# Differential attention and the latent branch's merge as one stage in half tiles, on one Trainium2 core

## The reference

```
z = h @ w_in                      # among others q_d, k_d, v_d and three gates of 1024 columns
p  = softmax(q_d[...,0] . k_d[...,0]) - lam * softmax(q_d[...,1] . k_d[...,1])   # 4 heads, 64 columns per map
o_d = rms(p @ v_d) * g * (1 - lam_init)                                           # per head of 128
y = sig(gate_m) * (o_m @ w_m) + sig(gate_a) * (o_a @ w_a) + sig(gate_d) * (o_d @ w_d)
x = x + g1 * (y @ w_out)          # then an MLP with squared ReLU
```

## Time and profile before

| what | value |
|---|---|
| median of three runs | 2680.42 us |
| profiled execution | 2682.99 us, span 2681.1 us, mean granted clock 0.983 |
| TensorE busy | 2559.7 us, 95% |
| VectorE busy | 1180.7 us, 44% |
| ScalarE busy | 744.2 us, 28% |
| GpSimd busy | 1330.8 us, 50% |
| da, layer 0 and layer 1 | from 585.2 and 1896.3 us, about 76 us each |

### The profile page before, as it was taken

How to read it: one execution, slowest core, us unless ns; L and a number is a source line. 1 busy time by engine, 2 the same in 40 slices (tenths; PEclk the granted TensorE clock), 3 DMA queues, 4 the chain that set the end, 5 groups by cost and what they waited for, 6 DMA issues and landing times.

```text
span 2681.1 us, 41661 instructions
## 1 busy us (share of the span) xinstructions
PE 2559.7 (95%) x17328; PEld 2394.0 (89%) x17328; DVE 1180.7 (44%) x1692; ACT 744.2 (28%) x1332; POOL 1330.8 (50%) x604
## 2 busy tenths in 40 slices
PE   4999989999999999999989999899999999999997
PEld 3989976877999999999978899668789999999997
DVE  4443265777224523132554523659742273132233
ACT  3251235225312312021222522450433123021121
POOL 2635530340566666666654356105236666666664
PEclk8999999999999999999998999999999999999999
DMA  6202224530222222222211122342012222222221
GB/s 249 70 24 70 73 79 158 195 111 9 72 71 71 71 79 72 77 73 73 78 55 55 32 74 71 117 158 79 32 40 71 73 70 71 79 72 78 72 78 57
DMA packets 62555, 215.33 MB, mean 80 GB/s; under 512 B 6688, under 2 KB 11168, under 8 KB 62112
## 3 DMA queue, kind: packets, MB, share of 16 engines
q1 hardware_dynamic: 56448, 203.97, 22.3%
q10 hardware_dynamic: 5920, 8.70, 0.9%
HBM read 208.15 MB, written 4.49 MB: 79 GB/s over the span
## 4 chain that ended last, share of the span: by engine, by line
PE 83%; DVE 8%; issue 3%; ACT 1%; DVEq 1%; POOL 1%; DMA 1%; SPq 1%; POOLq 0%; ACTq 0%
PE big L469 22%; PE big L473 22%; PE big L472 22%; PE big L620 4%; PE last_two L651 2%; PE two L634 2%; PE last_two L547 1%; PE big L493 1%; DVE cols L1377 1%; PE big L496 1%; PE big L497 1%; DMA first_mod<-in_first 1%; DVE sq L1720 1%; SPq L380 1%; DVE q_a L1684 1%
## 5 line engine op out<-in xcount | busy, mean ns | idle before, releaser
L437 POOL TENSOR_TENSOR w_hi<-raw,cst 128x1024 fp32r<-128x1024 f32 x288 | 556.1, 1931 | 1219.9 <-PE big L469 1106.8
L469 PE MATMUL big<-act_hi,w_hi 128*128 128x320 f32 x2784 | 870.5, 313 | 6.9 <-issue 5.6
L472 PE MATMUL big<-act_lo,w_hi 128*128 128x320 f32 x2784 | 864.5, 311 | 0.0
L473 PE MATMUL big<-act_hi,w_lo 128*128 128x320 f32 x2784 | 864.1, 310 | 0.0
L440 POOL TENSOR_TENSOR w_lo<-raw,w_hi 128x1024 fp32r<-128x1024 f32 x288 | 744.1, 2584 | 41.0
L469 PEld LDWEIGHTS big<-act_hi,w_hi 128*128 128x128 f32 x2784 | 526.6, 189 | 16.6 <-issue 14.8
L472 PEld LDWEIGHTS big<-act_lo,w_hi 128*128 128x128 f32 x2784 | 526.6, 189 | 1.0
L473 PEld LDWEIGHTS big<-act_hi,w_lo 128*128 128x128 f32 x2784 | 526.4, 189 | 0.0
L469 PE MATMUL big<-u_hi,w_hi 128*128 128x320 f32 (+1 forms) x1024 | 319.0, 312 | 2.0 <-DVE u_lo L1783 2.0
L472 PE MATMUL big<-u_lo,w_hi 128*128 128x320 f32 (+1 forms) x1024 | 317.4, 310 | 0.0
L473 PE MATMUL big<-u_hi,w_lo 128*128 128x320 f32 (+1 forms) x1024 | 317.0, 310 | 0.0
(11 more groups left out here) (306 smaller groups left out, 3456.9 us busy)
## 6 DMA issues: line engine op xcount, KB each, us to landing
raw<-in_w SPq DMA_DIRECT2D x368, 512.0 KB, 3.5
first_mod<-in_first SPq DMA_DIRECT2D x16, 512.0 KB, 15.8
x<-in_x ACTq DMA_DIRECT2D x1, 2560.0 KB, 12.9
out_y<-x SPq DMA_DIRECT2D x8, 320.0 KB, 2.3
cst<-in_const ACTq DMA_DIRECT2D x1, 1664.0 KB, 10.3
small<-in_small ACTq DMA_DIRECT2D x2, 437.0 KB, 9.5
out_C<-c_new ACTq DMA_DIRECT2D x2, 258.0 KB
v_d<-in_past ACTq DMA_DIRECT2D x2, 256.0 KB, 3.1
```

The lines of the kernel that those rows point to most:

```text
L437: nc.gpsimd.tensor_tensor(w_hi[:, to, :], raw[:, slot, :], ones[:, 0:1].to_broadcast([P, BLK]), ALU.mult)
L469: first = mm(ps, wh, ah, start=k == 0, stop=False)
L472: mm(ps, wh, al, start=False, stop=False)
L473: last = mm(ps, wl, ah, start=False, stop=k == nk - 1)
```

## The change

- merge_a is no stage of its own any more. Its 576 products are cut into half tiles: an item is one gate tile's half of 320 tokens (24 products) or one branch tile's half (12 products). They go to two PSUM banks of their own, one per half (`half_banks`). The products are dealt out over 42 slots: two ahead of and between the first scores, then two per unit.
- da gets its own loops on all engines (`attend_d`). Per unit TensorE makes the scores of unit i+1, a slot, the transposes of unit i, a slot, the values of unit i. The scores read 64 rows of q_d and k_d directly, the two maps alternating; q_map, its zeros and `lay_out` are gone. Transposes and values share two further banks, and VectorE copies each unit's output at once (`out_copied`).
- ScalarE takes tanh of each gate half in da (`half_gates`), VectorE multiplies and adds each branch half there (`half_branches`).
- The squares of the heads stand in da, in four tiles (`head_sq`). The sums, roots, scaling and splits stand beside the first gates of merge_d (`head_roots` for two heads at once). merge_d's order is four gates, four branch tiles, then twice two gates and two branch tiles, with the weight blocks put in that order; tanh has four tiles (`tanh_d`).
- In layer 0, the transposition of the next layer's second modulation chunk moves from behind dv's products to behind their second block.

The diff, cut to its core (the indentation is cut by eight; the latent attention's own `attend` loses its parameters and is otherwise the same):

```diff
+SOURCES = {"norm2": 0, "norm1": 8}
+N_SOURCES = 16
+PAIR_PRODUCTS = 6 * (2 * KD + 2 * 4)
+SLOTS = 2 * (5 * H_D + 1)
+def products_before(slot):
+    return 4 * PAIR_PRODUCTS * slot // SLOTS
+def half_tile(n):
+    p, r = divmod(n, PAIR_PRODUCTS)
+    if r < 12 * KD:
+return p, r // (3 * KD), r % (3 * KD)
+    return p, 4 + (r - 12 * KD) // 12, (r - 12 * KD) % 12
+def half_tiles_done(slot):
+    done = []
+    for n in range(products_before(slot), products_before(slot + 1)):
+p, item, at = half_tile(n)
+if at == (3 * KD if item < 4 else 12) - 1:
+    done.append((p, item))
+    return done
+GATE_USE_D = [0, 1, 2, 3, 8, 9, 12, 13]
+BRANCH_USE_D = [4, 5, 6, 7, 10, 11, 14, 15]
+GATE_BLOCK_D = [0, 1, 2, 3, 6, 7, 9, 10]
+BRANCH_BLOCK_D = [4, 5, 8, 11]
...
-q_map = [stage, sq]
...
+tanh_d = [stage[:, 0, :], stage[:, 1, :], prob_d[:, 2, :], prob_d[:, 3, :]]
+head_sq = [sq[:, 0, :], sq[:, 1, :], rs[:, :], prob_d[:, 0, :]]
...
+four = ctx.enter_context(nc.psum_tensor("four", [P, 4, 512], f32))
+two, last_two = four[:, 0:2, :], four[:, 2:4, :]
+one = [four[:, 2, :], four[:, 3, :]]
+half_banks = [four[:, 3, 0:HALF], four[:, 0, 0:HALF]]
+turned_d = four[:, 1:3, :].rearrange("p a c -> p (a c)")[:, 0:T]
+out_d = [four[:, 2, P:2 * P], four[:, 2, 2 * P:3 * P]]
...
+        name = "merge_d"
+        def gate(m):
+            project(l, USE[name][GATE_USE_D[m]:], FIRST_BLOCK[name] + GATE_BLOCK_D[m], 1, KD, act_hi, act_lo)
+        def branch(p):
+            project(l, USE[name][BRANCH_USE_D[2 * p]:], FIRST_BLOCK[name] + BRANCH_BLOCK_D[p], 2, 4, od_hi, od_lo,
+                    arrived=(lambda k: l * SPLITS + FIRST_SPLIT["od"] + k + 1) if p == 0 else None)
+        gate(0)
+        pe.wait_ge(out_copied, l * 20 + 20)
+        for b in range(2):
+            pe.wait_ge(half_free[b], l * 16 + 16)
+        head_sums(l, "dn", (0, 1))
+        gate(1)
+        head_sums(l, "dn", (2, 3))
+        gate(2)
+        gate(3)
+        branch(0)
+        branch(1)
+        for p in range(2, 4):
+            gate(2 * p)
+            gate(2 * p + 1)
+            branch(p)
+    def merge_a(l, slot):
+        for n in range(products_before(slot), products_before(slot + 1)):
+            p, item, at = half_tile(n)
+            m, h = divmod(item % 4, 2)
+            k, term = divmod(at, 3)
+            gate = item < 4
+            b = FIRST_BLOCK["merge_a"] + 3 * p + (m if gate else 2)
+            col = P * (k if gate else 4 * m + k)
+            hi, lo, nk = (act_hi, act_lo, KD) if gate else (oa_hi, oa_lo, 4)
+            begins = at == 0 and h == 0 and (gate or m == 0)
+            if begins:
+                block_start(l, b)
+            if at == 0 and n and not (p == 0 and item == 1):
+                pe.wait_ge(half_free[h], l * 16 + 4 * p + item // 2)
+            if p == 0 and item == 1 and at == 0:
+                pe.wait_ge(v_copied, l * 2 + 2)
+            if p == 0 and item == 4 and term == 0:
+                pe.wait_ge(lo_done, l * SPLITS + FIRST_SPLIT["oa"] + k + 1)
+            src = (w_hi, w_hi, w_lo)[term][:, b % SPLIT, col:col + P]
+            moving = (hi, lo, hi)[term][:, k, h * HALF:h * HALF + HALF]
+            one_product = mm(half_banks[h], src, moving, start=at == 0, stop=at == 3 * nk - 1)
+            if begins:
+                one_product.then_inc(block_used, 1)
+            if at == 3 * nk - 1:
+                one_product.then_inc(half_ready[h], 1)
+    def attend_d(l):
+        units = attention_units(H_D, 1)
+        n = len(units)
         def scores(i):
             h, t = units[i]
             q0, q1 = queries(t)
             k0, k1 = keys(t)
...
+            uses = USE["da"][2 * i:2 * i + 2]
+            for use in uses:
                 wait_free(pe, l, use)
...
+            w = (k1 - k0) // (1 if t == LATE else 2)
+            for c in range((k1 - k0) // w):
+                for m, use in enumerate(uses):
+                    ps, b, _ = buf(use)
+                    r = slice(64 * m, 64 * m + 64)
+                    last = mm(ps[:, c, 0:w], q_d[r, h, q0:q1], k_d[r, h, k0 + c * w:k0 + c * w + w],
                               start=True, stop=True)
...
+                    if c == (k1 - k0) // w - 1:
+                        last.then_inc(ready[b], 1)
         def turn(i):
             h, t = units[i]
...
+            pe.wait_ge(p_ready, l * 60 + 40 + i + 1)
             if i:
...
+                pe.wait_ge(out_copied, l * 20 + i)
+            src = prob_d[:, 2 * (i % 2), :]
+            for c in range(1 if t == LATE else 5):
+                last = nc.tensor.transpose(turned_d[:, P * c:P * c + P], src[:, P * c:P * c + P], ident)
+            last.then_inc(pT_ready, 1)
+        def values(i):
+            h, t = units[i]
+            pe.wait_ge(pT_copied, l * 60 + 40 + i + 1)
+            for c in range(1 if t == LATE else 5):
+                last = mm(out_d[i % 2], v_d[:, c if t == LATE else c + 1, P * h:P * h + P],
+                          probT_d[:, i % 2, c, :], start=c == 0, stop=c == (0 if t == LATE else 4))
+            last.then_inc(o_ready, 1)
+        merge_a(l, 0)
+        for i in range(-1, n):
+            if i + 1 < n:
+                scores(i + 1)
+            if i >= 0:
+                merge_a(l, 2 * i + 2)
+                turn(i)
+            merge_a(l, 2 * i + 3)
+            if i >= 0:
+                values(i)
...
         pe.wait_ge(past_loaded, l * 64 + 64)
-        attend(l, "da", 2, 1, 40, 4, lambda h, m: q_map[h % 2][:, m, :], lambda h, m: k_d[:, h, :],
-               lambda h, c: v_d[:, c, P * h:P * h + P], H_D, prob_d, probT_d)
-        def behind_pair_a(p):
-            if p == 0:
-                pe.wait_ge(o_copied, l * 16 + 16)
-            head_sums(l, "dn", (p,))
-        merge(l, "merge_a", oa_hi, oa_lo, "oa", None, behind_pair_a)
-        merge(l, "merge_d", od_hi, od_lo, "od")
+        attend_d(l)
+        merge_d(l)
...
+    def head_square(l, h):
+        act.wait_ge(out_copied, l * 20 + 5 * h + 5)
+        f(head_sq[h], q_d[:, h, :], ACT.Square).then_inc(sq_ready, 1)
+    def head_roots(l, name, heads):
+        for h in heads:
+            act.wait_ge(rs_used, l * N_NORMS + NORMS[name] + 1)
+            act.wait_ge(head_sum, l * 4 + h + 1)
...
                 behind(m)
...
+    def gate_of_d(l, m):
+        use = USE["merge_d"][GATE_USE_D[m]]
+        wait_ready(act, l, use)
+        act.wait_ge(y_done, l * 24 + 18 + max(m - 3, 0))
+        t, b, _ = buf(use)
+        f(two_parts(tanh_d[m % 4]), halves(t), ACT.Tanh, scale=0.5).then_inc(free[b], 1)
+        act.drain().then_inc(gate_ready, 1)
+    def half_gates(l, slot):
+        for p, item in half_tiles_done(slot):
+            if item >= 4:
+                continue
+            m, h = divmod(item, 2)
+            act.wait_ge(half_ready[h], l * 16 + 4 * p + m + 1)
+            if p:
+                act.wait_ge(half_merged, l * 16 + 4 * (p - 1) + item + 1)
+            f(stage[:, m, h * HALF:(h + 1) * HALF], half_banks[h], ACT.Tanh, scale=0.5).then_inc(half_free[h], 1)
+            act.drain().then_inc(half_gated, 1)
...
+            act.wait_ge(pT_ready, l * 60 + 40 + i + 1)
+            if i >= 2:
+                act.wait_ge(o_ready, l * 60 + 40 + i - 1)
+            w = CTX if t == LATE else T
+            f(probT_d[:, i % 2, :, :].rearrange("p c q -> p (c q)")[:, 0:w], turned_d[:, 0:w], ACT.Copy)\
+                .then_inc(pT_copied, 1)
+        for i in range(-1, n):
+            if i + 1 < n:
+                exps(i + 1)
+            if i >= 0:
+                half_gates(l, 2 * i + 2)
+                copyT(i)
+            half_gates(l, 2 * i + 3)
+            if i > 5 and i % 5 == 1:
+                head_square(l, (i - 6) // 5)
+        head_square(l, H_D - 1)
+    def attend(l, beside):
+        units = attention_units(H_A, 2)
...
+        attend_d(l)
         act.wait_ge(diff_stored, l * 32 + 32)
...
+        gate_of_d(l, 0)
+        head_roots(l, "dn", (0, 1))
+        for h in (0, 1):
+            head_hi(l, "od", q_d, od_hi, h)
+        gate_of_d(l, 1)
+        head_roots(l, "dn", (2, 3))
+        for h in (2, 3):
...
+    def merge_d(l, behind):
+        for m in range(8):
+            use = USE["merge_d"][BRANCH_USE_D[m]]
+            dve.wait_ge(gate_ready, l * 16 + 8 + m + 1)
+            wait_ready(dve, l, use)
+            t, b, _ = buf(use)
+            v.scalar_tensor_tensor(two_parts(t1[:, :]), two_parts(tanh_d[m % 4]), 1.0, halves(t), ALU.add,
+                                   ALU.mult).then_inc(free[b], 1)
+            dve.drain()
+            v.tensor_tensor(y[:, m, :], y[:, m, :], t1[:, :], ALU.add).then_inc(y_done, 1)
+            dve.drain()
+            dve.drain().then_inc(whole, 1)
+            behind(m)
+    def half_branches(l, slot):
+        for p, item in half_tiles_done(slot):
+            if item < 4:
+                continue
+            m, h = divmod(item - 4, 2)
+            z = slice(h * HALF, (h + 1) * HALF)
```

(98 more changed lines are left out.)

232 lines of the change are left out of this document (102 added, 130 removed).

## The result

The changed kernel takes 2666.67 us (median of 4 runs) against 2681.72 of the kernel before: ratio 0.9943, 95% interval 0.9931 to 0.9956, 15 us faster. I had forecast 35. Its profiled execution has a span of 2664.1 us (from the first to the last instruction), 17.0 less.

The account below looks back on a forecast made before the run. TensorE, busy 95% of the span, was taken as the bound. Per layer 135.2 own time + 8 stalls + 4.3 head sums = 147.5 us, against 165.2 and 164.4, saved 34.6: 2646 us, range 2622 to 2670.

Parts of the forecast that it names:

- the stage: From the first half product to merge_d's first gate, the fused stage; forecast at about 143 us.
- The stall term: VectorE's SBUF-only operations in the new stage standing still while GpSimd works: 8 us per layer, bounds 0 and 52.
- cover: Delay on VectorE hidden before TensorE waits: 1.9 us in a unit without a half branch, 0.6 with one.
- The lock itself: VectorE and GpSimd share an SBUF port pair exclusively; the loser blocks fully, hitting scaling, difference and add.
- TensorE's own time: TensorE's work in the new stage, products, scores, transposes and values: 135.2 us per layer.
- the rival with 15 us per layer: Stalls of 15 us per layer in the new stage, half buffers late as well: 2660 us, chance 0.19.
- no overlap: Rival: 64-row score halves don't run side by side in this order; 2663 us, chance 0.08.
- side-by-side row halves: 64-row scores of the two maps overlap on TensorE: four 320-column products two at a time, 1.07 us.
- merge_d's reordering: Four branch tiles in a row, one per 3.5 us, against VectorE's 0.82 + 0.88 us and drains: hidden.
- the hidden normalisation: Head normalisation beside merge_d's first four gates: done by 27.5 us, first branch at 32.5; unhidden, 1 or 2 us.
- the scores' 1.1 to 1.3 us: Sign that the forecast is right: a unit's scores in the new stage take this long; 2.15 us means wrong.
- the filling: Filling TensorE's idle holes in da, about 2.2 us per head, 9 us per layer; the smaller part on offer.

## Why the prediction was wrong

The direction was right, the size was not: 17.0 us of span instead of 34.6. Per layer the stage is 8.1 us longer than I had it; twice that is 16.2. The remaining 1.4 us lie outside the stage and can't be told from chance: in nine profiled executions, of the changed kernel and its variants, the stage of layer 0 begins between 581.3 and 584.2 us, though the program is the same up to there. Two terms of the sum failed, both too small.

- **The stall term**, 8 us, is 12.2, and it had the wrong cover. The lock itself behaved as said; the scaling, which has only one tensor operand, stands still too (0.61 to 2.25 us). But I gave 3.5 us to the gates and 6.2 to the branches, and by the table above gates lose 9.8 and branches 2.4. I priced each block's delay in a gate unit against 1.9 us of cover, which is VectorE's way to the output copy. The shorter way leads through the next maxima, the exponentials, tanh of a gate half and ScalarE's copy to the values. I had worked out its cover (0.3 to 0.8 us) and yet took 2 us off for it, where it should have raised the price. The three waits ahead of values, 3.5 us, are this way. Nor does a delay end with its unit: at the longest stall the late difference holds up a half branch, the output copy and the next maxima. I also left out what a stall does to the clock: about 1.25 + 0.5 us at the longest stall of a layer, which is inside the 12.2.
- **TensorE's own time**, 135.2, is 139.1 at most (the kernel with GpSimd's work taken out). Entering and leaving the 64-row form costs 0.4 per unit instead of 0.23: 16 x 0.17 + 4 x 0.11, some 3 us; the rest is handovers.

By its stalls, the rival with 15 us per layer (2660, a chance of 0.19) comes nearest, though its mechanism, late half buffers, is the smallest part: the two waits for a half bank in layer 0 are 0.92 and 0.38 us. By the time alone, "no overlap" (2663) is nearer to the measured 2666.67, and the scores of 1.28 us rule it out: two terms that were too small add up to about the same time. What I had right: side-by-side row halves, no gain from merge_d's reordering and no loss, the hidden normalisation, the scores' 1.1 to 1.3 us.

I also took the faster scores for the larger part and the filling for the smaller. The experiments show that the scores alone are worth nothing: in the two kernels with them da got longer, not shorter. In the fused stage the overlap of the row halves is worth 20 us (2686.9 against 2666.7). So the two work together: the products cover the chain over VectorE and ScalarE, and then the shorter scores shorten the sum that counts. What the filling is worth by itself stays open, since the kernel with slow scores also pays for the 64-row form.

## What to carry to other kernels

When a stage that GpSimd left alone gets work that GpSimd must prepare, look at which VectorE operations there read only SBUF, and at what moment. GpSimd's start is free to choose: a wait on the semaphore that ends VectorE's vulnerable stretch gave back 11.4 of 12.2 us per layer here, and the same wait one step earlier in the chain cost 4.2 us more. Price such a delay along every way that leads from VectorE back to TensorE, by the one with the least cover, and follow it into the next unit.

## Not expected of the hardware

- Two fp32 score tiles on different row halves overlap whether their products alternate in the queue or not (1.28 us both ways, 2.35 on the same rows).
- In the kernel before with faster scores, a stretch in which TensorE has only scores and waits had a granted clock of 0.61, though products filled the stretch before. In the changed kernel a wait of 2.51 us in a full stretch was followed by some 3.4 us at the lower level (0.93 over the 23.7 us of the window), and the waits of 1.30 us by none.
